# The scale of the first feed-forward's normalisation applied after its up projection instead of before it

## The reference, cut to what matters

```python
D_FF = 4 * D_MODEL          # 4096
EPS = 1e-5

def rmsnorm(x, w):
    xf = x.astype(jnp.float32)
    y = xf * lax.rsqrt(jnp.mean(jnp.square(xf), axis=-1, keepdims=True) + EPS)
    return (y * w.astype(jnp.float32)).astype(x.dtype)

def hybrid_layer(h, ...):
    ...                                           # mixers, then
    h = h + jnp.concatenate([o_gla, o_swa], axis=-1) @ w_out
    f = rmsnorm(h, norm_ff_w)
    return h + jnp.square(jax.nn.relu(f @ w_ff1)) @ w_ff2
```

## Time and profile before

| | |
|---|---|
| median of 3 runs | 2020.01 us |
| the profiled execution's own time | 2018.61 us |
| its span in the trace | 2016.6 us |
| PE busy | 1966.4 us, 98% |
| DVE busy | 1146.0 us, 57% |
| ACT busy | 787.8 us, 39% |
| POOL busy | 366.2 us, 18% |
| mean granted TensorE clock | 0.992 of full speed |

### The profile page before, as it was taken

The page is one execution under the profiler, slowest core; times in us unless marked ns, Lnnn a source line. Parts: engine busy times, 40 slices in busy tenths (PEclk is TensorE's granted clock), DMA queues, the critical chain, the costliest instruction groups (busy, mean ns, idle before and its releaser), DMA issues.

```text
span 2016.6 us, 25560 instructions
## 1 busy us (share of the span) xinstructions
PE 1966.4 (98%) x9548; PEld 1575.5 (78%) x9548; DVE 1146.0 (57%) x1757; ACT 787.8 (39%) x1332; POOL 366.2 (18%) x298
## 2 busy tenths in 40 slices
PE   8999999999999999999999999999999999999998
PEld 6876678888887788888888877777676788888887
DVE  7566667777667655453564265665535755354444
ACT  7437433222225222222332345557756442222223
POOL 3000039999200695000000000000001000000000
PEclk9999999999999999999999999999999999999999
DMA  6320146666432664333245433333125423332331
GB/s 167 88 70 22 53 132 206 204 199 210 123 94 64 178 198 144 97 90 104 83 124 134 120 110 110 109 96 125 54 89 190 121 82 96 92 104 86 101 98 59
DMA packets 274990, 233.13 MB, mean 116 GB/s; under 512 B 16631, under 2 KB 248442, under 8 KB 274368
## 3 DMA queue, kind: packets, MB, share of 16 engines
q1 hardware_dynamic: 255792, 166.29, 28.3%
q0 software_dynamic: 17488, 60.36, 9.6%
q10 hardware_dynamic: 1632, 5.45, 1.2%
HBM read 214.95 MB, written 12.58 MB: 113 GB/s over the span
## 4 chain that ended last, share of the span: by engine, by line
PE 89%; DVE 5%; ACT 3%; issue 1%; DMA 1%; ACTq 1%; DVEq 0%; POOLq 0%
PE bank L1131 25%; PE bank L1133 24%; PE bank L1132 24%; PE bank L1137 2%; PE bank L1138 2%; DVE wlo L1896 1%; PE bank L1655 1%; PE bank L1557 1%; PE bank L1672 1%; PE bank L1796 1%; PE bank L1813 1%; PE bank L1348 1%; PE bank L1187 1%; PE bank L1496 1%; DMA arena<-spill_pa 1%
## 5 line engine op out<-in xcount | busy, mean ns | idle before, releaser
L1131 PE MATMUL bank<-xhi,whi 128*128 128x512 f32 x1680 | 666.2, 397 | 6.1 <-PE bank L1672 2.2
L1133 PE MATMUL bank<-xhi,wlo 128*128 128x512 f32 x1680 | 656.0, 390 | 0.0
L1132 PE MATMUL bank<-xlo,whi 128*128 128x512 f32 x1680 | 654.9, 390 | 0.0
L1896 DVE TENSOR_TENSOR wlo<-stage,whi 128x1024 fp32r<-128x1024 f32 x309 | 407.4, 1329 | 208.7 <-ACT whi L558 208.4
L558 ACT ACTIVATE whi<-stage 128x1024 fp32r<-128x1024 f32 x309 | 321.2, 1051 | 411.2 <-PE bank L1133 373.2
L1131 PEld LDWEIGHTS bank<-xhi,whi 128*128 128x128 f32 x1680 | 316.1, 188 | 76.5 <-issue 9.3
L1133 PEld LDWEIGHTS bank<-xhi,wlo 128*128 128x128 f32 x1680 | 315.8, 188 | 68.0
L1132 PEld LDWEIGHTS bank<-xlo,whi 128*128 128x128 f32 x1680 | 316.4, 188 | 63.3
L2265 DVE SCALAR_TENSOR_TENSOR H<-bank,sc,H 128x512 f32<-128x512 f32 x304 | 217.7, 746 | 77.3 <-PE bank L1133 75.5
L1131 PE MATMUL bank<-hidhi,whi 128*128 128x512 f32 x532 | 209.3, 393 | 0.0
L1133 PE MATMUL bank<-hidhi,wlo 128*128 128x512 f32 x532 | 208.5, 392 | 0.0
(11 more groups left out here) (438 smaller groups left out, 2082.4 us busy)
## 6 DMA issues: line engine op xcount, KB each, us to landing
arena<-in_w_ada POOLq DMA_DIRECT2D x72, 512.0 KB, 4.0
stage<-in_w_in SPq DMA_DIRECT2D x71, 512.0 KB, 3.9
stage<-in_w_ff SPq DMA_DIRECT2D x64, 512.0 KB, 4.2
stage<-in_w_gate SPq DMA_DIRECT2D x44, 512.0 KB, 4.6
stage<-in_w_up SPq DMA_DIRECT2D x44, 512.0 KB, 3.8
stage<-in_w_down SPq DMA_DIRECT2D x44, 512.0 KB, 3.8
arena<-arena ACTq DMA_DIRECT2D x16, 256.0 KB, 5.5
stage<-in_w_proj_a SPq DMA_DIRECT2D x8, 512.0 KB, 4.0
```

Source lines behind the costliest of these rows:

```text
L1131: mm(out, sh, mh, start=start, stop=False, **kw)
L1132: mm(out, sh, ml, start=False, stop=False, **kw)
L1133: return mm(out, sl, mh, start=False, stop=stop, **kw)
L1896: V.tensor_tensor(wlo[:, static % SPLITS, :], stage[:, static % STAGES, :], whi[:, static % SPLITS, :].bitcast(F32), ALU.subtract).then_in ...
```

## The change

The first feed-forward's up product is now taken on `H * norm_ff_w` without 1/rms. ACT makes `xhi` from `H` with the gain as its scale, right after the squares; DVE makes `xlo` from `H`, the gain and `xhi` in one instruction. The tiles `u0` are no longer used here, nor are the semaphore steps on them. On PE the sums for 1/rms come after tile 2 of the first chunk and the spread after tile 6 (`between`); the six `idle_products` of this place are gone. On ACT the square root stands between `xhi` 4 and `xhi` 5; on DVE reciprocal and diagonal stand behind `xlo` 4, and after `xlo` 7 DVE waits for the spread factor and copies it from `bank[6]` to the SBUF tile `ff_rstd`. In all sixteen groups DVE now makes `act_t[j] = max(bank, 0) * ff_rstd` itself, and then `hid_t[j] = act_t[j] * act_t[j]`; ACT's relu is gone, and its square waits for DVE.

```diff
@@ -290,7 +290,7 @@
         SUM_NO = {1: 0, 3: 1, 4: 2, 5: 3, 6: 4}
         ONCE = {n: i + 1 for i, n in enumerate(("lam_exp", "silu_c", "softplus", "kdecay_ready", "kt_out", "ostd", "f_softplus", "em_ready"))}
         STD_NO = {0: 1, 1: 2, 3: 3, 2: 4, 4: 5, 5: 6, 6: 7}
-        split_seq = {k: n for n, k in enumerate([1, 3, 4, 5])}
+        split_seq = {k: n for n, k in enumerate([3, 4, 5])}
 
         gg = sb("gg", [P, 2, META + T])
         xrow = [tl(2 * b, 2) for b in range(NB)]
@@ -314,6 +314,7 @@
         ada_sum = gg[:, 0, 0:P]
         u0 = [tl(27 + k) for k in range(4)]
 
+        ff_rstd = tl(31)
         act_t = [tl(32), tl(33)]
         hid_t = [tl(34), tl(35)]
 
@@ -559,12 +560,12 @@
 
             act.dma_start(ident[:, :], t["c_ident"]).then_inc(s("ident_loaded"), 16)
 
-            def split_hi(n, kt, src, shift=0.0):
+            def split_hi(n, kt, src, shift=0.0, gain=1.0):
 
                 if n > 0 and kt == 0:
                     act.wait_ge(chunk_done, split_last[n - 1] + 1)
                 if isinstance(shift, float):
-                    ins = A_(xhi[:, kt, :], src, ACT.Copy)
+                    ins = A_(xhi[:, kt, :], src, ACT.Copy, scale=gain)
                 else:
                     ins = A_(xhi[:, kt, :], src, ACT.Identity, bias=shift)
                 ins.then_inc(s("x_rounded"), 1)
@@ -825,12 +826,15 @@
                 if c >= C_OUT1 + 2:
                     square(1, c - C_OUT1 - 2)
 
+            def raw_hi(kt):
+
+                act.wait_ge(H_added, norm_H[1] + kt + 1)
+                split_hi(split_no[1], kt, H[:, kt, :], gain=pc("norm_ff_w", kt))
+
             def ffn1_group(g, chunk, last=False):
 
                 hi(*chunk(0))
                 for j in range(2):
-                    act.wait_ge(chunk_done, 4 * g + (C_FF1 + j + 1))
-                    A_(act_t[j], bank[j][:, :], ACT.Relu).then_inc(act_fn, 1)
                     act.wait_ge(act_fn, 2 * g + (j + 1))
                     A_(hidhi[:, j, :], act_t[j], ACT.Square).then_inc(hid_rounded, 1)
                     hi(*chunk(1 + j))
@@ -855,7 +859,16 @@
                 if not last:
                     hi(*chunk(5))
 
-            norm(1, KT - 2)
+            A_(small[:, 255:256], eps[:, 0:1], ACT.Sqrt)
+            square(1, KT - 2)
+            raw_hi(0)
+            square(1, KT - 1)
+            for kt in range(1, 5):
+                raw_hi(kt)
+            act.wait_ge(s("sq_used"), STD_NO[1] - 1)
+            A_(std4, bank[7][:, 0:NB], ACT.Sqrt, scale=1.0 / D, bias=eps[:, 0:1]).then_inc(s("std_ready"), 1)
+            for kt in range(5, KT):
+                raw_hi(kt)
             ffn1_group(0, lambda j: (C_FF1 + j + AHEAD,))
             with act.Fori(0, (G_FF1 - 1) // 3 - 1) as i:
                 for m in range(3):
@@ -1205,7 +1218,7 @@
                 for semaphore, value in free:
                     pe.wait_ge(semaphore, value)
                 for n, kt in enumerate((0, KT - 1) if k in (1, 5) else (KT - 1, 0)):
-                    if n and k in (1, 5):
+                    if n and k == 5:
                         idle_products(1, 5)
                     if kt == 0:
                         pe.wait_ge(s("sq_summed"), 6 * SUM_NO[k] + 6)
@@ -1516,13 +1529,13 @@
                     pe.wait_ge(H_added, n - 3)
                 project(c, bank[n % 4][:, :], filling=1 if n == 0 else None).then_inc(chunk_done, 1)
 
-            def ffn_group(g, base, per, hb, hid0, first, filling=None, static=None, before_down=None, before_third=None, before_fourth=None):
+            def ffn_group(g, base, per, hb, hid0, first, filling=None, static=None, before_down=None, before_third=None, before_fourth=None, between=None):
 
 
                 n1 = per - 2
                 c0, st = (g * per + base), static
                 if first:
-                    project_two(c0, [bank[0][:, :], bank[1][:, :]], filling, 2 if n1 == 2 else 0)
+                    project_two(c0, [bank[0][:, :], bank[1][:, :]], filling, 2 if n1 == 2 else 0, between)
                 for j in range(2 if first else 0, n1):
                     if not first:
                         pe.wait_ge(H_added, g * 8 + (hb - 8 + 4 + j + 1))
@@ -1563,11 +1576,14 @@
 
             HID0 = {"FF1": 0, "FFA": 2 * G_FF1, "FFB": 2 * G_FF1 + 2 * G_FF2}
 
-            norm(1, [(s("sw_mix"), NB)])
-            idle_products(2)
-            spread(1)
-            idle_products(3)
-            ffn_group(0, C_FF1, 4, H_base["FF1"], 0, True, 2, C_FF1)
+            def first_scale(kt):
+
+                if kt == 2:
+                    norm(1, [(s("sw_mix"), NB)])
+                if kt == 6:
+                    spread(1)
+
+            ffn_group(0, C_FF1, 4, H_base["FF1"], 0, True, 2, C_FF1, between=first_scale)
             with pe.Fori(0, (G_FF1 - 1) // 3) as i:
                 for m in range(3):
                     ffn_group(i * 3 + (1 + m), C_FF1, 4, H_base["FF1"], 0, False, None, C_FF1 + 4 + 4 * m)
@@ -2278,11 +2294,14 @@
                     before_hidden()
                 for j in range(2):
 
-                    dve.wait_ge(act_fn, g * 2 + (hid0 + j + 1))
                     if per == 4:
-                        V.scalar_tensor_tensor(out=hid_t[j], in0=bank[j][:, :], scalar=0.0, in1=act_t[j],
-                                               op0=ALU.max, op1=ALU.mult).then_inc(hid_f32, 1)
+                        dve.wait_ge(chunk_done, g * per + (base + j + 1))
+                        V.scalar_tensor_tensor(out=act_t[j], in0=bank[j][:, :], scalar=0.0, in1=ff_rstd,
+                                               op0=ALU.max, op1=ALU.mult).then_inc(act_fn, 1)
+                        dve.wait_ge(act_fn, g * 2 + (hid0 + j + 1))
+                        V.tensor_tensor(hid_t[j], act_t[j], act_t[j], ALU.mult).then_inc(hid_f32, 1)
                     else:
+                        dve.wait_ge(act_fn, g * 2 + (hid0 + j + 1))
                         dve.wait_ge(chunk_done, g * per + (base + 2 * j + 2))
                         V.tensor_tensor(hid_t[j], bank[2 * j + 1][:, :], act_t[j], ALU.mult).then_inc(hid_f32, 1)
                     if per == 4:
@@ -2301,7 +2320,14 @@
 
             unit = lambda x: one_col
             ffn_chunk = lambda c: (c,)
-            norm(1)
+            for kt in range(KT):
+                dve.wait_ge(s("x_rounded"), 8 * split_no[1] + kt + 1)
+                V.scalar_tensor_tensor(out=xlo[:, kt, :], in0=H[:, kt, :], scalar=pc("norm_ff_w", kt), in1=xhi[:, kt, :].bitcast(F32),
+                                       op0=ALU.mult, op1=ALU.subtract).then_inc(x_ready, 1)
+                if kt == 4:
+                    rstd_diag(1)
+            dve.wait_ge(s("spread"), STD_NO[1] - 1)
+            link(V.tensor_copy(ff_rstd, bank[6][:, :]))
             ffn_group(0, C_FF1, 4, unit, lambda j: (C_FF1 + j + AHEAD,))
             with dve.Fori(0, (G_FF1 - 1) // 3 - 1) as i:
                 for m in range(3):
```

## The result

The changed kernel takes 2045.81 us (median of 4 runs, 2043.01 to 2046.75) against 2018.82 us for the kernel before in the same session: a ratio of 1.0127, 95% interval 1.0112 to 1.0142. It is 27 us slower; forecast were 2019.7 us and no change that can be measured.

The account below looks back on a forecast made before the run. PE was taken to bound the kernel. Start gain -2.25, clock +1.4, sixteen groups +1.0 and POOL's earlier start +0.9 sum to +1.05 us on 2018.61, giving 2019.7 us; range 2014.5 to 2026.

Parts of the forecast that it names:

- What bounds the kernel: Whole kernel: PE, busy 98% of the span; at the feed-forward's start a 7.4 us hole in its useful work.
- The start, undisturbed: Start of the first group: the new order brings the second `hidlo` to 286.5 against 288.76, a gain of 2.25 us.
- The clock: First chunks of the new order: one fall to half rate for about 3.4 us, costing 1.4 us; bounds 0 and 3.2.
- POOL's earlier start: First group: POOL's first scaling at 280.2 falls into DVE's chain, costing 0.9 us; bounds 0 and 3.5.
- Sixteen groups: Loop: the added square is exposed to POOL in eleven groups, costing 1.0 us; bounds a gain of 0.3 and 15.
- The slower one: Rival: square meets POOL's add in all eleven groups, 7.0 us, start gains nothing, 2025.6 us; chance 0.17.
- The other three: Rivals: handover gain arrives, 2016.7 us, chance 0.22; clock low for two lengths, 2021.5, 0.08; new waits not covered, 0.02.

Follow-up runs that it names:

- a_short_pool: The changed kernel with POOL's work on `w_ada_2` cut to 32 of 1024 columns for seven of eight tiles; 2013.61 us.
- b_short_pool: The kernel before with POOL's work on `w_ada_2` cut to 32 of 1024 columns for seven of eight tiles; 2014.60 us.
- a_psum_hid: The changed kernel with DVE's square fed from PSUM and its result kept in the PSUM bank, so `hidlo` has one SBUF input; 2019.39 us.
- a_pool_late: The changed kernel with POOL released only after the first group's two `hidlo`, some 10 us later; 2050.99 us.
- b_sbuf_square: The kernel before with one operand changed: `hid_t` = `act_t` * `act_t` instead of max(bank, 0) * `act_t`; 2029.01 us.
- a_lo_last: The changed kernel with the `wlo` between the two hidden blocks moved behind the second `hidlo`, in all sixteen groups; 2035.25 us.
- a_slack: The changed kernel with three down matmuls of block 0 put before block 1's on PE, so `hidlo` is needed 0.68 us later; 2042.61 us.
- b_extra_psum: The kernel before with one more DVE instruction per hidden block, ahead of `hid_t`, from PSUM into an unused tile (0.69 us); 2036.43 us.

## Why the prediction was wrong

- **What bounds the kernel** was right: PE, and at the start the hole in its useful work.
- **The start, undisturbed** was right to 0.2 us. Counted from the last add, with 3.68 us taken off the changed kernel's times: the first matmul at 266.73 (266.6 predicted), column sums at 270.35 (270.25), spread at 277.64 (277.6), POOL's first scaling at 280.22 (280.2). The undisturbed second `hidlo` came 2.44 us earlier (a_short_pool against b_short_pool; 2.25 predicted).
- **The clock** was wrong by its whole term at the start, 1.4 us. It did not fall over the first chunks of the new order:

```profile
270.00:282.00 12.00, 11.53 (x57) 9.10 (x57) 6.59 (x12) 6.34 (x11) 1.58 (x3) 1.00 0.09 15
```

It fell later, at 292.9 and 419.2, beside PE's waits for `hidhi` and `hidlo`. The prediction had no term for this; it cost 5.5 us in the loop. Its upper bound was also miscounted: 3.2 is half of 6.5 us, and less the 1.9 us of sums it would be 2.3.

- **POOL's earlier start**: 0.9 us was taken from an average hold of 0.37 times two or three instructions; the difference between the changed kernel and the one with POOL cut is 26.10 - 20.46 = 5.6 us. It lies above the upper bound of 3.5, which counted one scaling and one add; in fact DVE met a scaling and two adds (at 285.89, 287.83 and 292.81).
- **Sixteen groups** is the step that failed. The mechanism was named, with the rule of the Trainium skill ("SBUF — State Buffer", "Who interferes with whom") that a DVE instruction with two SBUF inputs and a GpSimd instruction reading SBUF exclude each other. The trace agrees with it: from 300 to 500 us `hidlo` took 2.41 with two SBUF inputs, 0.69 with one in the same place (a_psum_hid). The size was wrong: 1.0 us against 23.2, and even the bound of 15 (11 x 1.42 is 15.6) was too low, though only nine groups and a part of the tenth ran beside POOL. I had laid the new chain over the positions that POOL's instructions had in the old trace. These are not fixed. As I read the rows, POOL waits for DVE as DVE waits for POOL, so an exposed instruction of DVE sets where POOL's next one falls: behind the square, ahead of `hidlo`, in block 1 of nine groups out of nine. In all five kernels with such a square and full adds (the changed one, a_pool_late, b_sbuf_square, a_lo_last, a_slack) `hidlo` is 2.20 to 2.41; in none of the others is it above 1.62. I had also looked at block 1 alone. Holds of block 0 and of `wlo` move block 1's start, since DVE works in order; moving `wlo` away was worth 11.6 us, waits and clock together. And I priced a late `hidlo` by the wait alone, not by the clock that falls beside such waits.
- **The rivals.** The slower one was the right mechanism with its place, at 7 us instead of 23, and I gave only 0.05 to holds long enough for more than 0.5%. What speaks against it, "most positions miss it", is the sentence that the trace refutes. That the start gains nothing then was right in direction: it lost 3.2 us. The other three did not happen as told; the clock was low for two lengths, but beside the waits for `hidlo` and not over the first chunks.

What stays open: why 0.7 us more of immune work ahead of `hidlo` (b_extra_psum) raises its mean hold from 0.4 to 0.9 us was not shown step by step, nor why the four executions of a_slack fall into two pairs 10 us apart (mean granted clock 0.992 in the fast pair, 0.988 in the slow one). Both may be phases between two engines that wait for each other. No run here separates them further. Nor does a run show which waits of PE let the clock fall.

## What to carry to other kernels

Before an instruction is added to a chain of one engine, ask of each link which port or lock it shares with an engine that runs beside it, and count both the exposed links and the microseconds added ahead of one. Here a way of three immune links cost nothing (a_psum_hid). One operand that exposed a second link, with no time added, cost 9 us of loop (b_sbuf_square); 0.7 us of immune work put ahead of an exposed link cost 15 (b_extra_psum); the change did both, for 23. In this case the two engines fell into step, so positions read from the trace of before did not hold after the edit; bound the loss by one full hold for every exposed link in every repetition, including links earlier in the engine's order, and add what the clock takes when PE waits that long. If a link must stay, take its exposure away (an operand or the result left in PSUM) before trying to give it slack.

## What the runs showed of the hardware

- A DVE instruction can write its result over the PSUM bank that it reads, at the same price (0.699 us for 128x512), and a following one with that bank and one SBUF operand is not held by POOL (0.692 us beside POOL at work).
- One 128x1024 add of POOL (2.41 us alone) held a two-input DVE instruction by up to 2.2 us (`wlo` 3.41 for 1.23), and adds that began inside a square of DVE took 2.67 to 2.89 us. Between square and `hidlo` of block 1, dependent and both exposed, with a gap of 0.03 to 0.04 us in the trace, POOL got its turn in nine groups of nine.
- The granted clock stayed at the 2.4 GHz level through a stretch in which PE idled 1 us and then worked in bursts (the window row above), while at the same place in the kernel before, after the sums and empty matmuls, it had fallen. In the changed kernel it fell twice beside waits of PE of 2.0 to 2.2 us, for 6.8 us each, and PE then started 12 matmuls of 128x512 in 5 us instead of 24.
- The scatter of the kernel before goes with the clock: over its 99 runs that were measured with the experiments, the 28 with a mean granted clock of 0.992 took 2017.6 us on average, the six with 0.988 took 2023.6.
